# Recurrent stage of a hybrid decoder step: the last high split of a pair ahead of the group norm's root, the low split ahead of its reciprocal, the bonus through another buffer

## What is computed

```python
def step(S, inp):                       # per token and head
    r_t, w_t, k_t, v_t, av_t, bv_t = inp
    sa = jnp.einsum('bhvk,bhk->bhv', S, av_t)
    S = S * w_t[:, :, None, :] + sa[..., None] * bv_t[:, :, None, :] + v_t[..., None] * k_t[:, :, None, :]
    return S, jnp.einsum('bhvk,bhk->bhv', S, r_t)
...
mu = jnp.mean(y, axis=-1, keepdims=True)
var = jnp.mean(jnp.square(y - mu), axis=-1, keepdims=True)
yn = ((y - mu) * lax.rsqrt(var + GN_EPS)).reshape(B, T, W) * lnx_w + lnx_b
bonus = jnp.sum(r_h * k_h * r_k, axis=-1, keepdims=True) * v_h
out = (yn + bonus.reshape(B, T, W)) * g
```

## Time and profile before

| | |
|---|---|
| device time, three runs | 2414.34, 2416.34, 2416.50 us, median 2416.34 |
| the profiled execution | 2415.23 us, of which the profile's span is 2413.5 us |
| PE busy | 2351.0 us, 97% of the span |
| DVE busy | 1473.5 us, 61% |
| ACT busy | 879.6 us, 36% |
| POOL busy | 131.3 us, 5% |
| chain that ended last | PE 82%, DVE 10%, issue 4%, ACT 1%, DMA 1% |
| recurrent stage | about 550 to 1150 us; a pair takes some 75.1 us |

### The profile page before, as it was taken

One profiled execution on the slowest core, in us unless ns is written; L12 is line 12 of the kernel. 1 busy time (PEld: TensorE's weight loads), 2 busy tenths in 40 slices (PEclk: granted clock), 3 DMA queues, 4 the chain that ended last, 5 costly groups with the idle time before them and its releaser, 6 DMA issues.

```text
span 2413.5 us, 48839 instructions
## 1 busy us (share of the span) xinstructions
PE 2351.0 (97%) x19616; PEld 2252.7 (93%) x19616; DVE 1473.5 (61%) x2125; ACT 879.6 (36%) x1048; POOL 131.3 (5%) x203
## 2 busy tenths in 40 slices
PE   8999999999999999999999998999999999999999
PEld 6899989898888888888999988999999999999998
DVE  5644544566677666776535457665666666566676
ACT  6443344343332233322434344333333333333334
POOL 3000011000000010000001010000000000000003
PEclk9999999999999999999999999999999999999999
DMA  7554487342333243332445633444444444444443
GB/s 267 185 165 142 160 285 251 97 140 90 99 100 96 85 137 96 100 96 86 151 153 160 197 105 105 157 140 143 158 151 149 147 156 140 143 157 151 152 145 110
DMA packets 282189, 346.67 MB, mean 144 GB/s; under 512 B 6957, under 2 KB 240733, under 8 KB 280907
## 3 DMA queue, kind: packets, MB, share of 16 engines
q1 hardware_dynamic: 271883, 307.66, 39.6%
q0 software_dynamic: 9712, 36.30, 4.5%
q10 hardware_dynamic: 464, 0.79, 0.1%
HBM read 333.83 MB, written 10.89 MB: 143 GB/s over the span
## 4 chain that ended last, share of the span: by engine, by line
PE 82%; DVE 10%; issue 4%; ACT 1%; DMA 1%; DVEq 1%; SPq 0%; ACTq 0%
PE bank L246 19%; PE bank L255 19%; PE bank L247 19%; PE bank L227 4%; PE bank L229 4%; PE bank L228 4%; PE bank L1193 3%; DVE work L911 2%; ACT hi L211 1%; DVE lo L218 1%; PE bank L1210 1%; PE bank L511 1%; DVE work L1025 1%; PE bank L512 1%; PE bank L518 1%
## 5 line engine op out<-in xcount | busy, mean ns | idle before, releaser
L218 DVE TENSOR_TENSOR lo<-raw,hi 128x2048 fp32r<-128x2048 f32 x286 | 655.8, 2293 | 502.9 <-ACT hi L211 485.6
L246 PE MATMUL bank<-ah,hi 128*128 128x320 f32 x3200 | 957.4, 313 | 0.2 <-DVE al L532 0.2
L247 PE MATMUL bank<-al,hi 128*128 128x320 f32 x3200 | 945.9, 309 | 0.0
L211 ACT ACTIVATE hi<-raw 128x2048 fp32r<-128x2048 f32 x286 | 548.0, 1916 | 935.1 <-PE bank L255 681.1
L246 PEld LDWEIGHTS bank<-ah,hi 128*128 128x128 f32 x3200 | 601.0, 188 | 15.4 <-issue 13.3
L247 PEld LDWEIGHTS bank<-al,hi 128*128 128x128 f32 x3200 | 601.4, 188 | 0.4
L255 PE MATMUL bank<-ah,lo 128*128 128x320 f32 x3200 | 545.4, 311 | 2.5 <-DVE lo L218 2.5
L255 PEld LDWEIGHTS bank<-ah,lo 128*128 128x128 f32 x3200 | 486.4, 188 | 7.4 <-DVE lo L218 4.1
L227 PE MATMUL bank<-bh,hi 128*128 128x320 f32 x704 | 218.7, 311 | 0.2 <-DVE work L2410 0.2
L229 PE MATMUL bank<-bh,lo 128*128 128x320 f32 x704 | 217.5, 309 | 0.0
L228 PE MATMUL bank<-bl,hi 128*128 128x320 f32 x704 | 217.5, 309 | 0.0
(11 more groups left out here) (386 smaller groups left out, 2090.7 us busy)
## 6 DMA issues: line engine op xcount, KB each, us to landing
raw<-in_w_in SPq DMA_DIRECT2D x98, 1024.0 KB, 5.3
raw<-in_w_up SPq DMA_DIRECT2D x88, 1024.0 KB, 5.1
raw<-in_w_down SPq DMA_DIRECT2D x44, 1024.0 KB, 5.1
raw<-in_w_branch SPq DMA_DIRECT2D x24, 1024.0 KB, 5.5
raw<-in_w_out SPq DMA_DIRECT2D x16, 1024.0 KB, 5.4
raw<-in_w_mem_k SPq DMA_DIRECT2D x8, 1024.0 KB, 5.8
raw<-in_w_mem_v SPq DMA_DIRECT2D x8, 1024.0 KB, 5.2
work<-in_cache_mem_k POOLq DMA_DIRECT2D x8, 1024.0 KB, 6.0
```

Of the source, the lines that this page charges most:

```text
L211: act.activation(hi[c % NS][:, :], raw[c % 2][:, :], ACT.Copy).then_inc(S("hi_done"), 1)
L218: dve.tensor_tensor(lo[c % NS][:, :], raw[c % 2][:, :], hi[c % NS][:, :], ALU.subtract)\
L246: pe.matmul(out, w, xh[:, 8 * h + k, :], start=h + k == 0, stop=False)
L247: pe.matmul(out, w, xl[:, 8 * h + k, :], start=False, stop=False)
```

## The change

```diff
@@ -939,6 +939,8 @@
                 tt(c5(t_rt), c5(t_ad), bmid(m_id[:, :], NC), ALU.add)
+                dve.wait_ge(S("turned_out"), OUT0_A + N_OUT_A * i + OUT_A["bonus"] + 1)
+                tt(bon, t_ck, row_(i + 16), ALU.mult)
                 plain(t_a2, "A2")
                 plain(t_b2, "B2")
@@ -948,8 +950,6 @@
                 weights_low(0)
                 plus(t_rt, "RT1")
                 plain(t_bd, "B4")
-                dve.wait_ge(S("turned_out"), OUT0_A + N_OUT_A * i + OUT_A["bonus"] + 1)
-                tt(bon, bon, row_(i + 16), ALU.mult)
                 prepare_norm(dve, vv, i + 1)
@@ -1000,9 +1000,9 @@
                 prepare_kk(dve, vv, i + 2)
-                prepare_rest(dve, vv, i + 1)
                 dve.wait_ge(S("y_ps"), i + 1)
                 vv.do(dve.tensor_copy(y_, bank[6][:, 0:T]), "y_out")
+                prepare_rest(dve, vv, i + 1)
                 ps("g")
@@ -1020,12 +1020,12 @@
                 prepare_ops(dve, vv, i + 1)
+                weights_low(5)
                 branch(1, 1)
                 dve.wait_ge(S("gn_sqrt"), i + 1)
                 vv.do(dve.reciprocal(ysq, ysq))
                 tt(ym, ym, ysq, ALU.mult)
                 tt(row_(i), ym, bon, ALU.add, "gated_out")
-                weights_low(5)
@@ -1046,8 +1046,7 @@
                 i = j - 1
                 ps("bonus")
-                act.wait_ge(S("gated_out"), j)
-                aa.do(act.activation(bon, pbank("bonus")[:, 0:T], ACT.Copy), "turned_out")
+                aa.do(act.activation(t_ck, pbank("bonus")[:, 0:T], ACT.Copy), "turned_out")
@@ -1083,7 +1082,7 @@
             if ps:
-                ps("mean")
+                ps("tr0")
                 act.wait_ge(S("ring_out"), OUT0 + N_OUT * j)
                 aa.do(act.activation(ysq, ysq, ACT.Sqrt), "gn_sqrt")
```

## The result

The changed kernel takes 2436.89 us (median of four runs, 2435.85 to 2439.19) beside 2416.39 us for the kernel before in the same comparison: 0.88% slower, ratio 1.0088 with a 95% interval of 1.0071 to 1.0106. The forecast of 2423.8 us had the sign right and the size far too small, and the time lies beyond its range of 2417 to 2431 us. The profiled execution took 2439.19 us, its span is 24.0 us longer than that of before.

A forecast was written before the change was run, and what follows sets the result against it. It took PE as the bound, held at seams by DVE's unbroken chain from line 1010 to the copy of "A2". Seven seams +6.0, first pair +0.7, end +0.8: +7.5 us on 2416.34 gives 2423.8 us, range 2417 to 2431.

The forecast's parts named there:

- The rival of 2406.2 us: At the seams: ACT's root is the only bound, so PE gains 1.28 + 0.27 us each; chance 0.10.
- the lower ends: Rival: the loop's branch takes little more than a gap, the bonus product 0.52 us; +3.3 us, 2419.6 us; chance 0.15.
- low split in: DVE's low split placed ahead of `branch(1, 1)` adds 2.28 us at each seam.
- gated row to the next pair's first copy: Low split gone from the pair's end: loop branch exposed, 0.50 us left instead of 2.40, net -1.90 us a seam.
- bonus product ahead of "A2": DVE's bonus product before the copy of "A2" adds 0.75 us a seam, bounds 0.52 to 0.88 for the product.
- copy of y first: DVE's copy of y ahead of `prepare_rest` removes PE's wait at "g", gaining 0.27 us for each pair.
- wait ahead of "A2": New PE wait for DVE's masked copies of "ABs" in seven seams, 1.1 to 1.4 us.
- wait ahead of "BCt": PE's wait at the seams for DVE's copy of "A2" (line 915) grows from 1.3 to 2.0 to 2.2 us.
- first pair's wait for line 915: In the first pair, an eighth PE wait for DVE's copy of "A2" appears, some 0.7 us.
- wait for a high split behind the last pair: Behind the last pair, PE's wait for a low split goes; one of 3 to 4 us for ACT's high split comes.
- a seam's sum: Net of DVE's moved operations at the start of "BCs": +0.86 us a seam, bounds 0.25 to 1.1.
- the first rival: Longer PE waits lower its clock at seams, at most 1.5 us each: 2429 us, or 2434 in all seven; chance 0.25.

The follow-up runs named there:

- filled again: Changed kernel plus idle products, without start flag, in PE's waits ahead of "A2" and behind "B2" at the seven seams: 2421.89 us.
- filled kernels: Two versions of the changed kernel with idle products in both PE waits at seven seams: 2421.26 us with the start flag, 2421.89 us without.
- y first: Kernel before, with only DVE's copy of y moved ahead of `prepare_rest`: 2410.79 us, ratio 0.9976.
- bonus only: Kernel before, with only the bonus through `t_ck` without waiting for the gated row, its product ahead of the copy of "A2": 2438.16 us.

## Why the prediction was wrong

**The bound was named rightly.** The gain of 1.28 us at "beCt" didn't come; PE met DVE's copies of "ABs" at "A2" in all seven seams. The rival of 2406.2 us is out, and the lower ends with it.

**The terms of the sum**, each read off after or an experiment:

| term | forecast | measured |
|---|---|---|
| low split in | +2.28 us | 780.00 - (777.09 + 0.49) - 0.12 = +2.30 |
| gated row to the next pair's first copy | 0.50 | 0.49 |
| bonus product ahead of "A2" | +0.75 | 1.38 - 0.62 = +0.76 |
| copy of y first | -0.27 | -0.52 to -0.71, mean -0.57 |
| wait ahead of "A2" | 1.1 to 1.4 | 1.66 to 1.86 |
| wait ahead of "BCt" | 2.0 to 2.2 | 2.06 |
| first pair's wait for line 915 | 0.7 | 0.8 (filled again) |
| wait for a high split behind the last pair | 3 to 4 | 3.54 |

Two were mis-sized. The copy of y brought twice its term, because I took idle time as it is printed, from modelled ends. With it a seam's sum is +0.6 us instead of +0.86, and the filled kernels show 75.77 - 75.25 = +0.52, which is 3.6 us in seven seams instead of 6.0. The wait ahead of "A2" was worked out from the bonus part alone, where it did measure 1.3 us; the splits put 2.30 - 1.91 = 0.39 us more on DVE between line 1010 and "ABs", which I had in the sum at "BCs" but not in this wait. 1.3 + 0.4 is what was found, to 0.13 us at this seam and 0.25 or less at the others. The exposed branch agrees with the 0.3 us between the rows of the sequencer (in after they start at 784.6 and 784.9), and not with the 108 ns that the Trainium skill gives (Advanced Engine Details and Errata, Control Flow Timing).

**The step that failed** is the price of the clock at the seams. The sum of +0.86 us at a seam has no term for it; it was left to the first rival, with a chance of 0.25, "three or four seams" in the range, and the sentence "A drop costs at most the 1.5 us seen". The clock fell at all seven seams and cost 2.2 us at each, 15 us of the 20.5, where the moved operations that the sum did price cost 4.6 to 5.2 instead of 7.5. That the sign came out right owes little to the sum: most of the loss came by the rival. Three parts of it went wrong:

- *How many seams.* I laid each new wait by itself between one of 1.88 us that kept the clock and one of 2.48 us that lost it, each seen once, and took their pairing ("only 1.38 us of small products between them") as a remark. The runs show that alone they lose it at 3 and at 6 of 7 seams, and together at all. A wait of 1.8 us with one of 1.3 us close behind it also loses it at all seven. And the two rows were no bracket: behind the same wait of 2.48 us the clock stayed at 1.00 in y first, and behind one of 2.47 us in bonus only.
- *How much.* I took the one drop that I had seen as the most that one can cost. With only the wait of 1.8 us open each drop cost 1.5 us, but with the one of 2.06 us open up to 2.5 (a seam of 78.30 us beside one of 75.77), and in after 1.2 to 2.7 us against the filled kernels' 75.77. In after the clock was already 0.50 during the second wait, and the full work behind it still ran at a mean of 0.72 for six us.
- *The wrong length for the first wait*, 1.1 to 1.4 instead of 1.8 us, which by itself made the rival look weaker.

The prediction weighed the Trainium skill's rule (TensorE: Matmul & The Clock Gate, Part 1) that idleness is judged by a count that runs freely. The pair of equal waits of 2.06 us with either outcome agrees with it. But I read it as "some seams drop and others don't", and in after all seven dropped.

**The end.** The high split's wait came as forecast, and the clock fell behind it (0.50 from 1181.2). By the spans the end costs more than the +0.8 us of the sum: of the 6.1 us by which the span of filled again is longer, 3.6 are the seams, 0.8 the first pair and 0.2 stood ahead of the stage, which leaves 1.5 us; the same account of after leaves 1.7. But the six kernels with this order at the end take from 1278.0 to 1280.2 us from the last "g" on, 2 us apart with the same orders there, so an end dearer than forecast isn't shown. With seams short of the forecast the whole is 4.6 to 5.2 us.

**What stays open.** What decides between two equal single waits wasn't tried. The 2.2 us per seam is a difference of whole kernels; at the seam shown the filler cost PE nothing of its own. That single waits of both lengths mattered was seen in one profiled execution of each; the spread of the runs of one of them says that its count changes from run to run.

## What to carry to other kernels

A wait that is taken away uncovers the next bound, so add up the other engine's work between two handovers before moving anything: here ScalarE's wait hid a VectorE without a pause, and shortening VectorE's chain by 1.2 us won more than removing any wait. Look at TensorE's waits at a handover together, not one by one: where they were harmless, lengthening them or bringing a second one close took the clock down, at three times the price of the moved operations. One execution in which a wait kept or lost the clock is one draw and no bound. To tell the two apart, fill the waits with products that nobody reads and see whether the time falls.

## What of the hardware was not expected

- TensorE doing idle products is faster overall than TensorE waiting: 2421.9 against 2436.9 us with the same VectorE order.
- The granted clock is no function of a wait's length: 1.77 us kept it and 1.65 us lost it in one kernel, 2.06 us did both in another, and 2.48 us lost it in the kernel before and kept it in y first. Two waits of 0.75 and 1.13 us close together lost it once. In the kernel with both waits it was 0.50 over three us and had a mean of 0.72 over the six that followed, with TensorE busy.
- Idle time printed for TensorE is too small by the overlap of consecutive groups, about 0.16 us here, and the first group behind a wait is a little longer, 0.11 us: a printed 0.27 us was 0.53 us of time.
- A product with a start flag into unused columns of a bank restarts what is being summed in the others. The Trainium skill says so (PSUM — Partial Sum Buffer, The four PSUM rules: the flag's effect spans the whole bank in the quadrants that it writes), and the two filled kernels agree: the branch sums change with the flag and stay what they were without it.
